# A four-layer hybrid trunk on one core: the first x and weights in pieces, and two weight splits and the rope moved in attention

## The reference

```python
hn = rms_norm(h, mix_norm_w)
q, k_c, v_c, k_s, v_s, k_w, v_w, g = split(hn @ w_in)         # 16 heads of 64, 4 key/value groups
q  = partial_rope(rms_norm(q, q_norm), pos)                   # rotates the first 16 of 64 dims
kc, vc = compress(k_c), compress(v_c)                         # silu(blocks @ w1 + b1) @ w2, 31 blocks of 32 tokens
kc = partial_rope(rms_norm(kc, k_norm[0]), pos[block_end])
ks = partial_rope(rms_norm(k_s, k_norm[1]), pos)
kw = partial_rope(rms_norm(k_w, k_norm[2]), pos)
o  = g0 * attend(q, kc, vc) + g1 * attend(q, ks, v_s) + g2 * attend(q, kw, v_w)   # causal softmax each
h  = h + o @ w_out
# partial_rope: x1, x2 = x[0:8], x[8:16];  (x1*cos - x2*sin, x2*cos + x1*sin)
```

## Time and profile before

| | |
|---|---|
| median of 3 runs | 1568.55 us (1567.23 to 1568.96) |
| the profiled execution | 1567.98 us, span 1566.1 us |
| TensorE busy | 1494.7 us, 95% of the span |
| VectorE, ScalarE, GpSimd busy | 863.1, 576.5, 290.0 us |
| granted TensorE clock, mean | 0.987 of full |
| first real matmul; first scores of attention | 12.91 us; 107.78 us |
| attention's groups | about 108 to 174, 241, 307 and 385 us |

### The profile page before, as it was taken

The page is one execution under the profiler, slowest core; times in us unless marked ns, Lnnn a source line. Parts: engine busy times, 40 slices in busy tenths (PEclk is TensorE's granted clock), DMA queues, the critical chain, the costliest instruction groups (busy, mean ns, idle before and its releaser), DMA issues.

```text
span 1566.1 us, 19940 instructions
## 1 busy us (share of the span) xinstructions
PE 1494.7 (95%) x7469; PEld 1212.5 (77%) x7469; DVE 863.1 (55%) x1119; ACT 576.5 (37%) x864; POOL 290.0 (19%) x325
## 2 busy tenths in 40 slices
PE   6979899899999999999999999998999999999999
PEld 4768777677788888788788867776787888887887
DVE  4546767665544444333397758989646444444222
ACT  4446666554423222222233353344333222232110
POOL 4154443400300000000000025666212000000000
PEclk9989999999999999999999999999999999999999
DMA  8200100111232222332232220111122223222232
GB/s 318 81 28 1 55 28 28 64 72 58 78 107 87 100 100 87 108 108 94 94 108 81 83 105 27 55 54 39 69 81 81 95 93 107 83 105 93 95 107 80
DMA packets 19737, 130.68 MB, mean 83 GB/s; under 512 B 2272, under 2 KB 2912, under 8 KB 5088
## 3 DMA queue, kind: packets, MB, share of 16 engines
q1 hardware_dynamic: 19536, 127.80, 23.1%
q10 hardware_dynamic: 144, 2.10, 0.4%
HBM read 127.79 MB, written 2.10 MB: 83 GB/s over the span
## 4 chain that ended last, share of the span: by engine, by line
PE 80%; POOL 9%; issue 6%; DVE 2%; ACT 1%; POOLq 0%; DVEq 0%; ACTq 0%
PE ps L431 22%; PE ps L432 22%; PE ps L433 22%; PE ps L732 4%; POOL Lx L2034 3%; PE ps L712 2%; PE ps L692 2%; POOL sqacc L1940 1%; POOL sm L1926 1%; POOL xdd L2029 1%; PE ps L636 1%; PE ps L637 1%; POOL xdt L2026 1%; PE ps L708 1%; POOL qn L1978 1%
## 5 line engine op out<-in xcount | busy, mean ns | idle before, releaser
L1386 DVE TENSOR_TENSOR wl<-wraw,wh 128x2048 fp32r<-128x2048 f32 x113 | 263.6, 2333 | 236.8 <-ACT wh L999 236.6
L431 PE MATMUL ps<-xh,wh 128*128 128x512 f32 (+2 forms) x912 | 359.1, 394 | 6.8 <-DVE xl L1396 3.4
L433 PE MATMUL ps<-xh,wl 128*128 128x512 f32 (+2 forms) x912 | 356.1, 390 | 0.0
L432 PE MATMUL ps<-xl,wh 128*128 128x512 f32 (+2 forms) x912 | 355.9, 390 | 0.0
L999 ACT ACTIVATE wh<-wraw 128x2048 fp32r<-128x2048 f32 x113 | 215.5, 1907 | 186.7 <-PE ps L433 177.8
L431 PEld LDWEIGHTS ps<-xh,wh 128*128 128x128 f32 (+2 forms) x912 | 170.6, 187 | 44.9 <-issue 4.5
L433 PEld LDWEIGHTS ps<-xh,wl 128*128 128x128 f32 (+2 forms) x912 | 170.5, 187 | 37.3
L432 PEld LDWEIGHTS ps<-xl,wh 128*128 128x128 f32 (+2 forms) x912 | 170.5, 187 | 36.7 <-issue 0.7
L431 PE MATMUL ps<-hh,wh 128*128 128x512 f32 x352 | 137.9, 392 | 4.1 <-DVE hid L1471 4.1
L432 PE MATMUL ps<-hl,wh 128*128 128x512 f32 x352 | 137.8, 391 | 0.0
L433 PE MATMUL ps<-hh,wl 128*128 128x512 f32 x352 | 137.6, 391 | 0.0
(11 more groups left out here) (274 smaller groups left out, 2444.6 us busy)
## 6 DMA issues: line engine op xcount, KB each, us to landing
wraw<-wstream SPq DMA_DIRECT2D x113, 1024.0 KB, 4.7
cw<-cw_in SPq DMA_DIRECT2D x1, 4096.0 KB, 18.6
xT<-xT_in SPq DMA_DIRECT2D x4, 512.0 KB, 8.1
part<-xT_in ACTq DMA_DIRECT2D x1, 2048.0 KB, 7.6
out<-xT SPq DMA_DIRECT2D x8, 256.0 KB, 6.5
rows<-rows_in SPq DMA_DIRECT2D x1, 276.0 KB, 10.7
tri<-tri_in SPq DMA_DIRECT2D x1, 192.0 KB, 9.9
cmask<-cmask_in SPq DMA_DIRECT2D x1, 128.0 KB, 10.1
```

Source lines behind the costliest of these rows:

```text
L431: mm(o, wa[0], xa[0], start=start, stop=False)
L432: mm(o, wa[0], xa[1], start=False, stop=False)
L433: return mm(o, wa[1], xa[0], start=False, stop=stop)
L1386: TTo(wl[:, s, :], wraw[:, s, :], wh[:, s, :].bitcast(F32), ALU.subtract).then_inc(lo_done, 1)
```

## The change

- x comes in 8 pieces of one k-tile, chunk 0 in 4 pieces of one k-tile (512 columns) and chunk 1 in 2 halves. ACT and DVE split them piece by piece.
- PE does six float32 matmuls on zeros first (POOL writes the zeros), then goes through chunks 0 and 1 k-tile by k-tile, over all four token tiles each, where before it went token tile by token tile. `column_sums(0)` comes behind both.
- ACT does one small copy before it waits for anything.
- SP waits for the low parts of chunks 0 and 1 and issues chunks 2 and 3 ahead of `cw1` and `cw2`.
- The gates' product moves ahead of the transposes of `kvc` and into PSUM bank 6; `gates_f` is copied by ACT ahead of the taps, and PE's third and fourth transposes wait for that copy.
- On DVE `split_lo(2)` moves ahead of `mean_square(0)`, `split_lo(3)` ahead of the tap copies, and `split_lo(4)` between the two halves of `tbT`.
- In attention one split moves from step 14 to 13, the other from step 0 to 1.
- The rope's four products of 48 elements become two of 96; its subtraction and addition stay.

The diff, without the lines that only declare semaphores and the shape of `rp`:

```diff
...
 @block.sync
 def _(sp):
     sp.dma_start(cols[:, :], cols_in).then_inc(cols_landed, 16)
-    for k in range(4):
-        sp.dma_start(xT[:, 2 * k:2 * k + 2, :], xT_in[:, 2 * k:2 * k + 2, :]).then_inc(x_landed[k], 16)
-        if k == 0:
-            sp.dma_start(wraw[:, 0, :], wstream[0]).then_inc(landed[0], 16)
-    sp.dma_start(wraw[:, 1, :], wstream[1]).then_inc(landed[1], 16)
+    for k in range(KT):
+        sp.dma_start(xT[:, k, :], xT_in[:, k, :]).then_inc(x_landed[k], 16)
+        if k < 4:
+            sp.dma_start(wraw[:, 0, k * 512:(k + 1) * 512], wstream[0][:, k * 512:(k + 1) * 512]
+                         ).then_inc(quarter_landed[k] if k < 3 else landed[0], 16)
+    for k in range(2):
+        w = slice(k * 1024, (k + 1) * 1024)
+        sp.dma_start(wraw[:, 1, w], wstream[1][:, w]).then_inc(landed[1] if k else half_landed, 16)
     sp.dma_start(tri[:, :, :], tri_in).then_inc(params_landed, 16)
     sp.dma_start(ident[:, :], ident_in).then_inc(params_landed, 16)
     sp.dma_start(rows[:, :], rows_in).then_inc(params_landed, 16)
     sp.dma_start(posi[:, :], pos_in).then_inc(rest_landed, 16)
     sp.dma_start(cmask[:, :, :, :], cmask_in).then_inc(rest_landed, 16)
+    for k in range(2):
+        sp.wait_ge(lo_done, 1 + k)
+        sp.dma_start(wraw[:, k, :], wstream[2 + k]).then_inc(landed[k], 16)
     sp.dma_start(cw1[:, :, :, :], cw1_in).then_inc(cw_landed, 16)
     sp.dma_start(cw2[:, :, :, :], cw2_in).then_inc(cw_landed, 16)
     def chunk_pair(i, shift):
...
             sp.wait_ge(lo_done, 2 * i + (k - 1))
             sp.dma_start(wraw[:, k, :], wstream[bass.ds(2 * i + (k - shift), 1)].rearrange("a p n -> p (a n)")
                          ).then_inc(landed[k], 16)
-    with sp.Fori(1, (NS + 4) // 2) as i:
+    with sp.Fori(2, (NS + 4) // 2) as i:
         chunk_pair(i, 0)
     for k in range(NS + 3 - (NS + 3) % 2, NS + 4):
         sp.wait_ge(lo_done, k - 1)
...
         residual(down, hs, ready=lambda: pe.wait_ge(hl_done, hidden))
-    chunk_T(0, None, 0, range(4), 512, True, False, each=fresh(0))
+    pe.wait_ge(warm_zeroed, 1)
+    for _ in range(6):
+        mm(ps[:, 5, 0:256], qA[:, 0, 0:P].bitcast(F32), qA[:, 0, 0:256].bitcast(F32), start=True, stop=True)
+    for kt in range(4):
+        pe.wait_ge(xl_done, kt + 1)
+        if kt < 3:
+            pe.wait_ge(quarter_lo, kt + 1)
+        else:
+            pe.wait_ge(lo_done, 1)
+        w = slice(kt * 512, (kt + 1) * 512)
+        for tt in range(TT):
+            t = slice(tt * P, (tt + 1) * P)
+            ins = split_product(ps[:, tt, :], (xh[:, kt, t], xl[:, kt, t]), (wh[:, 0, w], wl[:, 0, w]), kt == 0,
+                                False)
+            if kt == 3 and tt % 2:
+                ins.then_inc(products, 1)
+    for kt in range(4, 8):
+        pe.wait_ge(xl_done, kt + 1)
+        pe.wait_ge(half_lo if kt < 6 else lo_done, 1 if kt < 6 else 2)
+        w = slice((kt - 4) * 512, (kt - 3) * 512)
+        for tt in range(TT):
+            t = slice(tt * P, (tt + 1) * P)
+            ins = split_product(ps[:, tt, :], (xh[:, kt, t], xl[:, kt, t]), (wh[:, 1, w], wl[:, 1, w]), False,
+                                kt == 7)
+            if kt == 7 and tt % 2:
+                ins.then_inc(products, 1)
     pe.wait_ge(params_landed, 48)
     column_sums(0)
-    chunk_T(1, None, 0, range(4, 8), 512, False, True, each=fresh(0))
+    narrow(CHUNK["gates"], 48, 6)
     for kv in range(2):
         for gp in range(2):
+            if kv == 1 and gp == 0:
+                pe.wait_ge(gates_out, 1)
             for tt in range(TT):
                 pe.wait_ge(evac, tt + 1)
                 f = kv * 256 + gp * P
                 ins = pe.transpose(ps[:, 4 + 2 * kv + gp, tt * P:(tt + 1) * P], kvc[:, tt, f:f + P],
                                    ident[:, :])
             ins.then_inc(kvT, 1)
-    pe.wait_ge(tb_act, 2)
-    pe.wait_ge(tb_vec, 2)
-    narrow(CHUNK["gates"], 48, 4)
     for k in range(2):
         chunk_T(CHUNK["qkv"] + k, None, 0, range(4 * k, 4 * k + 4), 512, k == 0, k == 1)
         if k == 0:
...
         residual(down)
+    act.wait_ge(mhalf_set, 1)
+    A(stat[:, 40:48], mhalf[:, :], ACT.Copy)
     act.wait_ge(cols_landed, 16)
     for kt in range(KT):
-        if kt % 2 == 0:
-            act.wait_ge(x_landed[kt // 2], 16)
+        act.wait_ge(x_landed[kt], 16)
         x_hi(0, kt)
-        if kt == 1:
-            split_hi(0)
+        if kt < 4:
+            w = slice(kt * 512, (kt + 1) * 512)
+            act.wait_ge(quarter_landed[kt] if kt < 3 else landed[0], 16)
+            A(wh[:, 0, w], wraw[:, 0, w], ACT.Copy).then_inc(quarter_hi if kt < 3 else hi_done, 1)
     square(0, 0, None, 0, 0)
     square(1, 0, None, 0, 0)
-    split_hi(1)
+    for k in range(2):
+        w = slice(k * 1024, (k + 1) * 1024)
+        act.wait_ge(landed[1] if k else half_landed, 16)
+        A(wh[:, 1, w], wraw[:, 1, w], ACT.Copy).then_inc(hi_done if k else half_hi, 1)
     for kt in range(2, KT):
         square(kt, 0, None, 0, 0)
     split_hi(2)
...
         act.wait_ge(products, 2 * 1 + 1 + tt // 2)
         A(kvc[:, tt, :], ps[:, tt, :], ACT.Copy, scale=stat[:, 24 + tt:25 + tt]).then_inc(evac, 1)
     split_hi(3)
+    act.wait_ge(products, 2 * CHUNK["gates"] + 2)
+    A(gates_f[:, :], ps[0:48, 6, :], ACT.Copy).then_inc(gates_out, 1)
     for kv in range(2):
         for gp in range(2):
             act.wait_ge(kvT, 2 * kv + gp + 1)
             for lp in range(2):
                 A(tb2[lp * DH:(lp + 1) * DH, kv, gp * 2 + 1, :], ps[DH:P, 4 + 2 * kv + gp, lp::2], ACT.Copy
                   ).then_inc(tb_act, 1)
-    act.wait_ge(products, 2 * CHUNK["gates"] + 2)
-    A(gates_f[:, :], ps[0:48, 4, :], ACT.Copy).then_inc(gates_out, 1)
     split_hi(4)
     act.wait_ge(angles_done, 1)
     A(sinT[:, :, :], ang[:, 8, :].rearrange("p (t f) -> p t f", f=8), ACT.Sin).then_inc(sincos_done, 1)
...
     dve.wait_ge(cols_landed, 16)
     for kt in range(KT):
-        if kt % 2 == 0:
-            dve.wait_ge(x_landed[kt // 2], 16)
+        dve.wait_ge(x_landed[kt], 16)
         x_lo(0, kt)
-        if kt == 1:
-            split_lo(0)
-    split_lo(1)
+        if kt < 4:
+            w = slice(kt * 512, (kt + 1) * 512)
+            if kt < 3:
+                dve.wait_ge(quarter_hi, kt + 1)
+            else:
+                dve.wait_ge(hi_done, 1)
+            TTo(wl[:, 0, w], wraw[:, 0, w], wh[:, 0, w].bitcast(F32), ALU.subtract
+                ).then_inc(quarter_lo if kt < 3 else lo_done, 1)
+    for k in range(2):
+        w = slice(k * 1024, (k + 1) * 1024)
+        dve.wait_ge(hi_done if k else half_hi, 1 + k)
+        TTo(wl[:, 1, w], wraw[:, 1, w], wh[:, 1, w].bitcast(F32), ALU.subtract).then_inc(lo_done if k else half_lo, 1)
     dve.wait_ge(params_landed, 48)
     dve.tensor_copy(ident_bf[:, :], ident[:, :]).then_inc(masks_cast, 1)
     step(TTo(diag[:, 0, :], tri[:, 1, :], ident[:, :], ALU.add))
     TS(negmask_bf[:, :], diag[:, 0, :], -NEG, NEG, ALU.mult, ALU.add).then_inc(masks_cast, 1)
+    split_lo(2)
     mean_square(0)
-    split_lo(2)
+    split_lo(3)
     for kv in range(2):
         for gp in range(2):
             dve.wait_ge(kvT, 2 * kv + gp + 1)
             for lp in range(2):
                 dve.tensor_copy(tb2[lp * DH:(lp + 1) * DH, kv, gp * 2, :], ps[0:DH, 4 + 2 * kv + gp, lp::2]
                                 ).then_inc(tb_vec, 1)
-    split_lo(3)
     dve.wait_ge(tb_vec, 8)
     dve.wait_ge(tb_act, 8)
     V.inc(dve.memset(tbT[:, :, :, :, :].rearrange("p k j g c -> p (k j g) c")[:, :, NCMP:32], 0.0))
...
             src = tb2[:, kv, :, 8 * jh:8 * jh + 248].rearrange("p g (c j) -> p j g c", j=8)
             pe_ = col(COL_PE + kv * NJ + 8 * jh, 8).unsqueeze(2).unsqueeze(3).broadcast_to([P, 8, GROUPS, NCMP])
             TTo(tbT[:, kv, 8 * jh:8 * jh + 8, :, 0:NCMP], src, pe_, ALU.add).then_inc(tbT_done, 1)
-    split_lo(4)
+        if kv == 0:
+            split_lo(4)
     dve.wait_ge(rest_landed, 32)
     step(dve.tensor_copy(stat[:, 16:21], posi[:, :]))
...
             qk_mean_square(TILE_MEAN.index(s), g + 1)
         if g < GROUPS - 1 and s == 8:
             stage_cmp_keys(g + 1)
-        if g < GROUPS - 1 and s == 14:
+        if g < GROUPS - 1 and s == 13:
             split_lo(n0 + 2 * g + 4)
-        if 1 <= g < GROUPS and s == 0:
+        if 1 <= g < GROUPS and s == 1:
             split_lo(n0 + 2 * g + 3)
         if S in (STEPS - 7, STEPS - 3, STEPS):
             split_lo(NS + 4 - (STEPS - S + 1) // 4)
...
         pool.wait_ge(ready, value)
         n = src.shape[-1]
         TTo(dst, src, mhalf[:, 0:n], ALU.pow).then_inc(done, 1)
+    pool.memset(qA[:, 0, 0:256].bitcast(F32), 0.0).then_inc(warm_zeroed, 1)
     pool.memset(mhalf[:, :], -0.5).then_inc(mhalf_set, 1)
     pool.wait_ge(mhalf_set, 1)
...
         q6 = qn[:, tt, :, 0, :]
         step(TTo(q6, proj[:, tt, 0:6, :], sm[:, 3, 0:6].unsqueeze(2).broadcast_to([P, 6, DH]), ALU.mult))
```

(24 more changed lines are left out.)

## The result

The changed kernel took 1542.48 us (median of 4 runs, 1541.77 to 1543.65) against 1568.33, a ratio of 0.984 with a 95% interval of 0.982 to 0.985. That is 25.9 us less; the prediction said 30 less (1538) and a range of 1530 to 1554. The profiled execution took 1541.77 us, span 1540.0. One execution of one experiment (the filled wait) ran at a granted clock of 0.849 and took 1674.79 us; it is left out of every comparison.

What follows compares the result with a forecast made beforehand. TensorE, busy 95% of the span, was taken as the bound, with gains only where it waits or its clock falls. Front 13.7 + joins 16.8 = 30.5 us off 1567.98 gave 1537.5, forecast 1538, range 1530 to 1554.

Steps and rivals of the forecast that it cites:

- The start of the front: Kernel start: x0 lands at 5.3 us, TensorE starts at 7.4, 5.5 earlier; column sums at 29.7 without waiting.
- the clock step: Kernel start: zero matmuls raise TensorE's clock by 7.4 us, leaving 0.5 us of slow matmuls; bounds 0 and 2.8.
- The chain behind it: After column sums: chunk 3 split at 38.8 us, VectorE's list to 55.2, GpSimd's first norm at 60.8 instead of 73.24.
- the whole front: Kernel start to the first query transposes: 12.4 us from the earlier first norm plus 1.3 from the rope, 13.7 us.
- the compression weights: Front transfers: issued at about 17.6 us instead of 7.2, landing by 36, wanted only at 61.
- The rope: GpSimd's norms: two products of 96 elements at 0.37 us each; 0.3 us less a norm, 1.3 in the front.
- The joins: Three joins between attention groups: moved VectorE splits stop stretching GpSimd's rstd and copy; 6.1 + 4.3 + 6.4 = 16.8 us.
- The second rival: Joins: norm's copy collides with the second split every time; 9.8 us less gain, 1548, or 1554; chance 0.18.

Runs made afterwards that it cites:

- the filled wait: Changed kernel plus ten constant float32 matmuls, results unused, in TensorE's wait before the first query transposes; three executions 1534.2 to 1538.0 us, ratio 0.981.

## Why the prediction was right, and where it was off

**The start of the front was right**: x0 at 5.3 (5.33), first product at 7.4 (7.69) at full spacing, column sums without a wait at 29.7 (29.56). The run without zero matmuls shows what the clock step rested on: cold, it would have been 2 us, inside the 0 to 2.8 I had bounded. That x0 came within 0.1 us is partly luck: in the twelve profiles with the small pieces ScalarE starts on it between 4.4 and 5.5 us, and the column sums start between 29.0 and 29.9 in those with the zero matmuls.

**The chain behind it was right in order and nearly in size**: chunk 3 split at 38.8 (38.39), VectorE's list to 55.2 (54.6), first norm at 60.8 (59.97). That the whole front agrees to 0.7 us (13.7 and 14.4) is partly luck too, since two executions of the old front are 2.1 us apart. One term was mis-sized without effect: the compression weights were issued at 20.1 us, not 17.6. That the order of the transfers was a part of this I had listed as cover only ("wanted at 61"); the cover that mattered was another, chunk 2's landing ahead of the mean square, and it is worth 5.5 us of the front.

**The rope was right in the front** (0.3 us a norm, 1.1 us in all, 1.3 forecast; a product of 96 elements took 0.39 us, 0.37 forecast). With the splits where the change puts them it is too small to show in the time.

**The joins were right in size, and right in a cause that is not the only one.** 16.8 was forecast, 16.4 came, and the splits' moves alone bring 16.1. But I took them for the only thing that would do. With the splits left in place the joins still give 10, because the shorter rope puts the copy ahead of the second split. I had computed where the copy ends in the new kernel, but not by how little it had lost the race in the old one: the copy's start (168.86) stood in the earlier trace rows, the split's (168.57) only in the trace. The second rival's mechanism, the copy colliding with a split, is real: it is what moving the first split alone runs into. It did not occur in the change: 1.1 us lie between the copy's end and the split at each of the three joins.

**The step that was off is the clock behind TensorE's waits**, a term that the sum did not have. After the front I let attention start as early as the transposes; but the clock, low behind the wait in both kernels, rose later in the profile of the change, 1.7 us. The wait grew from 6.4 to 7.3 us, but that this is the reason is not shown: behind 7.36 us the products took 2.26 us, behind 6.45 they took 3.62. And I took the clock's state elsewhere as unchanged. In the profiled execution two other waits, of 1.3 and 2.0 us, equally long in both kernels, were followed by a cold stretch after the change and not before, 1.6 us each. The second run of the same kernel without these two shows that the order of work does not decide them. What does is not shown. The forecast's 1538 lies 1 us from the median of that second run (1538.95) and 4.5 from the first's. 30.5 + 0.7 (front) - 0.4 (joins) - 1.7 - 1.6 - 1.6 = 25.9, with 26.1 measured in the spans.

## What to carry to other kernels

Where VectorE and GpSimd interleave on SBUF data, compare when the two operations start, not only how long they are: here a lead of 0.3 us decided about two, so two unrelated edits can be the same gain, and one edit alone (the first split) can lose what it should have helped. When summing a change by landmarks, give TensorE's short waits a term for the clock with a range (here 0 or 1.6 us each), and read one landmark in several executions before crediting an edit with 2 us. Where a wait can't be removed, try constant matmuls in it; here they gave 2.7 us at the next landmark, the reordering of the angles about 1. And a move into VectorE's idle time was not free where GpSimd was busy: 6.7 us instead of 2.6.

## What the runs showed of the hardware

Some VectorE operations on 40 columns took 1.16 to 1.30 us instead of 0.18 to 0.20 while GpSimd added 512-column tiles; GpSimd's eight additions kept their 13.2 us. The Trainium skill ("SBUF — State Buffer", Who interferes with whom) says that the shared ports are locked for whole instructions; the trace agrees, since a short operation waits out the rest of a long one.

TensorE's granted clock fell from 2.4 to 1.2 GHz behind a wait of 1.31 us in five of fourteen profiles and held behind the same wait in nine. After 5.2 to 8.5 us of idle ahead of the first transposes it was low in all twelve profiles that had such a wait; after 0.91 and 0.76 us it held.

The first piece of x, at the same place in the queue, took 3.2 to 4.3 us from its issue until ScalarE started on it with 256 KB (twelve profiles) and 4.3 and 4.9 with 512 KB (two): halving it saved some 0.8 us, about as much as one execution differs from the next.
